# Every third group of value pages summed by VectorE instead of TensorE in the chunk loop of a hybrid decoder step

## Chip, cores and metric

One Trainium2 chip, one core. The metric is the device time of one execution of the whole program in microseconds; lower is better.

## What is computed

The kernel does one inference step of a two-layer decoder for a prompt group (1024 tokens) and eight sample rows with a past of 2048 tokens each. Two parts of the first layer matter here. The samples attend to a paged cache, and the last product of that attention is a weighted sum of 16 value pages of 128 rows for every sample:

```python
k_past = k_pool[page_table].reshape(db, past, HA, 2, DA)
v_past = v_pool[page_table].reshape(db, past, HA, DVA)
...
return jnp.einsum('bhqk,bkhe->bqhe', a.astype(v.dtype), v)
```

The prompt goes through a gated delta rule in chunks, where each chunk needs the inverse of a unit lower triangular matrix and then passes a state on:

```python
v_new = u_c - w_c @ S
o = q_c @ S + attn_c @ v_new
S = S * jnp.exp(gl)[..., None, None] + jnp.einsum('bhck,bhcv->bhkv', k_c, v_new)
```

All is in 32-bit floats.

## The kernel before

The five engines each run one instruction list written out by hand, held together by semaphores. The names: H = 4 heads, NB = 8 chunks of 128 tokens, PG = 16 pages per sample, B = 8 samples, so 128 value pages in all. A group is STRIPS = 4 pages. There are GROUPS = 3 x NB = 24 groups in the chunk loop, which is pages 0 to 95 (samples 0 to 5, LATE = 96). The last 32 pages (samples 6 and 7) are summed in the output projection behind it.

**The chunk loop** (`chunk_pe` from L1890, `chunk_act`, `chunk_dve`) interleaves two chunks in step k = 1 to 8. It finishes the inverse of chunk k-1 (levels 3, 4, 5) and starts that of chunk k (levels 0, 1, 2). A level has a left product on PE, a scaled copy of it on ScalarE (`copy_x`), two right products on PE (`right`, `right_turned`), and two merges on VectorE (`join`, `join_turned`). With the inverse done, chunk k-1 gets its new values (L2012), ScalarE's copy of them (L2177), its outputs (L2022, L2023), the product for the state (L2032) and VectorE's state update (`advance`, L2330). Behind the update come the turned merge of level 2, the mask product `lower` (L2255) for the next chunk, ScalarE's seeds, and the first merge of the next step (`pairs`). PE's keys-times-state product (L2002) waits for the update and the seeds. In step 8 there is no chunk 8, so its levels 0 to 2 are left out, and gates and scales of the first output tiles stand in their place on VectorE (L1785, L1790).

**The value pages** ride along. SP loads pairs of pages into a ring of four slots (`load_pages`, issued at L1142, queued in order), each behind the use of the pair four earlier; `vpage_used` counts pages used, and starts at 8. `page_group` (L1848) sums four pages on PE: four matmuls, each with a page's 128x32 weights on its own 32 columns of the array and the page's 512 values as the moving operand, into one PSUM bank. `group_copy` (L1861 copies, L1864 adds) takes the bank into the sample's `strip_sum` on VectorE. Each step has three such groups: one behind the turned keys, one behind left(k, 1), and the third behind left(k, 2), directly ahead of the outputs. When a sample's four groups are in, `page_column` (L1835) folds the strips into one column per head, four products of a 128x128 stationary operand with one column, in steps 2, 4, 5, 6 and 8 (`SAMPLE_AT`), ahead of right_turned(k, 1). The column of sample 5 stands behind the first output job. `page_column_in` (L1868) copies a column out.

**Behind the loop**, `page_sum` (L1405 for a first page, L1407 for the others) sums the pages of samples 6 and 7 on VectorE: four multiply-adds of 128x128 per page, one per head, into an accumulator `pacc`. SP's list there is: two pairs of pages, then the parked residual (L1823, L1825), which waits for the last state update, then the other pairs with output weights (L1813) between them. PE runs the output jobs (L2406, eight 128x344 products of two passes each); job J waits for VectorE's addition (L2543) of job J - 4, and between the jobs stand small products such as L1774 and L2426.

Of the kernel before, what the change touches and what calls it, by code (L numbers as in the profile page):

```python
# [40 lines left out]
PG = 16  # L41
# [128 lines left out]
def build(nc, a, o):  # L170

    with ExitStack() as ctx:
# [6 lines left out]
        bank = ctx.enter_context(nc.psum_tensor("bank", [P, 8, 512], F32))  # L179
# [1213 lines left out]
        def page_sum(dve, g):  # L1393

            b, pp, u = g // PG, g % PG // 2, g % 2
            if u == 0:
                dve.wait_ge(page_in[pp % 4], b * 64 + (512 + 32 * (pp // 4 + 1)))
            dve.wait_ge(vpage_used, 8 + g)
            dve.sem_inc(wait_carrier, 1)
            for h in range(H):  # L1400
                v = (ring if b < B - 2 else ring_last)[:, pp % 4, u, h * P:(h + 1) * P]
                at = g * H + h
                w, d = aw_flat[:, at:at + 1], pacc[b - LATE // PG][:, h, :]
                if g % PG == 0:
                    last = dve.tensor_scalar(d, v, w, None, ALU.mult)  # L1405
                else:
                    last = dve.scalar_tensor_tensor(d, v, w, d, ALU.mult, ALU.add)  # L1407
            last.then_inc(vpage_used, 1)
# [170 lines left out]
        def over(where, n):  # L1579
            return where[:, 512 * n:512 * (n + 1)].rearrange("p (h t) -> p h t", h=H)  # L1580
# [13 lines left out]
        vb = [rb4(14), rb4(15)]  # L1594
        tmp_flat = tmp[:].rearrange("p s c -> p (s c)")
        k_last = big[:, 7 * TT:7 * TT + T]
        pacc = [over(k_last, 0), over(k_last, 1)]
        ring_last = tiles(0, 4)[:, :, 0:T].rearrange("p s (u n) -> p s u n", u=2)
        rows_first = wring[:, 0, 0:H, :]
        rows = [prod[:, 512 * n:512 * (n + 1)].rearrange("p (h t) -> p h t", h=H) for n in range(2)]  # L1600
# [21 lines left out]
        STRIPS = 4  # L1622
# [2 lines left out]
        SAMPLE_AT = {2: 0, 4: 1, 5: 2, 6: 3, 8: 4}  # L1625
        group_in = sem("group_in")
        strip_sum = [flat(16 * TT, H, P), flat(16 * TT + 512, H, P)]

        KK, QK, VT, KT = 1, 2, 3, 4

# [194 lines left out]
            sp.dma_start(res_b[:, k0:KD, chunk(c)], src[:, k0:KD, chunk(c)]).then_inc(x_back, 16)  # L1825

        def page_column(pe, b, n):
            strips = b < LATE // PG
            if strips:
                pe.wait_ge(group_in, PG // STRIPS * (b + 1))  # L1830
            else:
                pe.wait_ge(vpage_used, 8 + PG * (b + 1))
            part = strip_sum[b % 2] if strips else pacc[b - LATE // PG]
            for h in range(H):
                mm = pe.matmul(bank[:, n, h:h + 1], part[:, h, :], fold[:, h:h + 1] if strips else ones[:, 0:1], start=True, stop=True)  # L1835
            mm.then_inc(samp_full, 1)

        def page_group(pe, g, n):

            b, at = g * STRIPS // PG, g * STRIPS  # L1840
            for q in range(STRIPS):
                pp, u = (at + q) % PG // 2, q % 2
                if u == 0:
                    pe.wait_ge(page_in[pp % 4], b * 64 + 512 + 32 * (pp // 4 + 1))
            for q in range(STRIPS):
                pp, u = (at + q) % PG // 2, q % 2
                w = aw_flat[:, (at + q) * H:(at + q) * H + 32]
                mm = pe.matmul(bank[32 * q:32 * (q + 1), n, :], w, ring[:, pp % 4, u, :], start=True, stop=True)  # L1848
            mm.then_inc(vpage_used, STRIPS)

        def group_copy(dve, g, n):

            b = g * STRIPS // PG
            dve.wait_ge(vpage_used, 8 + STRIPS * (g + 1))
            d, src = strip_sum[b % 2].rearrange("p h e -> p (h e)"), bank[:, n, :]
            if g % (PG // STRIPS) == 0:
                if b >= 2:
                    dve.wait_ge(samp_full, b - 1)
                else:
                    dve.wait_ge(bias_io, 64)  # L1860
                dve.tensor_copy(d, src).then_inc(group_in, 1)  # L1861
            else:
                dve.wait_ge(group_in, g)
                dve.tensor_tensor(d, d, src, ALU.add).then_inc(group_in, 1)  # L1864

        def page_column_in(dve, b, n):
# [17 lines left out]
        def chunk_pe(pe):  # L1884
# [55 lines left out]
            def first(c):  # L1940
                if not live(c):
                    return
                pe.wait_ge(inv0, c + 1)
                if c >= 2:
                    pe.wait_ge(inv_up[c % 2], ps(c - 2, NL - 1, True))
                    pe.wait_ge(group_in, 3 * (c - 1))
                for h in range(H):
                    mm = pe.transpose(own(c, 1)[:, h, :], inv[c % 2][:, h, :], ident[:, :])
                mm.then_inc(m0_full, 1)
# [104 lines left out]
            for k in range(1, NB + 1):  # L2054
# [41 lines left out]
                    pe.wait_ge(x_copied[(k - 1) % 2], xs(k - 1, NL - 1))  # L2096
                    page_column(pe, SAMPLE_AT[k], 2 * ((k + 1) % 2))
                right_turned(k, 1)
                pe.wait_ge(group_in, 3 * k - 2)
                values_new(k - 1)  # L2100
                left(k, 2)
                page_group(pe, 3 * (k - 1) + 2, 2 * ((k - 1) % 2) + 1)
                pe.wait_ge(group_in, 3 * k - 1)
                outputs(k - 1)
                right(k, 2)
                right_turned(k, 2)
# [128 lines left out]
        def chunk_dve(dve, step):  # L2235
# [118 lines left out]
            for k in range(1, NB + 1):  # L2354
# [19 lines left out]
                group_copy(dve, 3 * (k - 1) + 1, 6)  # L2374
                join(k, 1)
                join_turned(k, 1)
                join(k, 2)
                advance(k - 1)
                join_turned(k, 2)
                lower(k + 1)  # L2380
                group_copy(dve, 3 * (k - 1) + 2, 2 * ((k - 1) % 2) + 1)
                if k in SAMPLE_AT:
                    page_column_in(dve, SAMPLE_AT[k], 2 * ((k + 1) % 2))

# [1473 lines left out]
```

## Time and profile before

| | us |
|---|---|
| median of 3 runs (2678.0 to 2679.62) | 2678.15 |
| the profiled execution | 2680.63 |
| its span | 2678.8 |
| PE busy in the span | 2628.7 (98%) |
| VectorE busy | 1524.4 (57%) |
| ScalarE busy | 1143.8 (43%) |
| GpSimd busy | 1349.5 (50%) |

The span is the time between the first and the last instruction in the trace. PE is TensorE's matmuls and PEld its weight loads; DVE is VectorE, ACT is ScalarE, POOL is GpSimd and SP is the engine that issues most DMAs (SPq is its queue). A matmul of 32-bit floats shows as two instructions, so a group of four is "x8". PE is busy for 98% of the span, but that is an average over stages: the long matmul streams of the later layers fill most of the span, and the chunk loop with its many short waits takes from about 572 to 745 us. What a change in the chunk loop is worth is read from that stretch and from the output projection behind it, 744 to 877 us.

### The profile page before, as it was taken

The page shows a single profiled execution, that of the slowest core. Times are in us where ns is not written, and L with a number is a line of the kernel's source. Part 1 is how long each engine was busy: PE and PEld are TensorE (multiplying, and loading weights), DVE is VectorE, ACT ScalarE, POOL GpSimd, SP SyncE. Part 2 cuts the span into 40 slices and gives each one's busy share as a digit, 9 for nine tenths or more (in the row PEclk, how much of TensorE's full clock was granted, in tenths as well). Part 3 has the DMA queues.
Part 4 walks back from the last instruction along what each step waited for, and adds up shares of the span by engine and source line. Part 5 has one row for each costly group of instructions (what it writes and reads, how often), then busy time and mean ns, then how long its engine had stood idle before and what let it go on. Part 6 is the DMA issues. An engine that isn't in the chain of part 4 may idle for free.

```text
span 2678.8 us, 46845 instructions
## 1 busy us (share of the span) xinstructions
PE 2628.7 (98%) x17261; PEld 2397.3 (89%) x17261; DVE 1524.4 (57%) x2930; ACT 1143.8 (43%) x1771; POOL 1349.5 (50%) x613
## 2 busy tenths in 40 slices
PE   8999999989999999999999999999999999999998
PEld 5886666667766999999999999999999999999998
DVE  4227868865567333333337885378863788635323
ACT  2227739955523433333233434344343433444333
POOL 0210015611001666667666677676866767665753
PEclk9999999989999999999999999999999999999999
DMA  5220057635683544444444444544444444444553
GB/s 184 69 95 9 17 167 220 206 97 157 174 274 115 149 137 139 142 142 142 141 142 131 138 142 133 144 141 134 142 126 142 142 137 140 134 133 135 155 153 95
DMA packets 457192, 369.00 MB, mean 138 GB/s; under 512 B 15501, under 2 KB 400114, under 8 KB 456732
## 3 DMA queue, kind: packets, MB, share of 16 engines
q1 hardware_dynamic: 444846, 347.05, 44.0%
q0 software_dynamic: 2992, 12.26, 1.5%
q10 hardware_dynamic: 9174, 7.22, 0.9%
q8 instruction: 122, 2.00, 0.3%
q14 instruction: 58, 0.48, 0.1%
HBM read 351.17 MB, written 17.14 MB: 137 GB/s over the span
## 4 chain that ended last, share of the span: by engine, by line
PE 69%; DVE 3%; ACT 1%; DMA 1%; issue 1%; POOL 0%; SPq 0%; DVEq 0%; ACTq 0%
PE bank L2914 21%; PE bank L2916 21%; PE bank L2915 21%; PE bank L2406 4%; DVE tmp L2782 1%; DVE bank L3495 1%; PE bank L1957 1%; ACT tmp L2774 1%; DMA big<-in_cache_attn_v 1%; DMA wring<-in_ffn_w_up 0%; PE bank L2790 0%; PE bank L1848 0%; PE bank L1774 0%; PE bank L3698 0%; POOL wl L3373 0%
## 5 line engine op out<-in xcount | busy, mean ns | idle before, releaser
L3373 POOL TENSOR_TENSOR wl<-wring,wh 128x1024 fp32r<-128x1024 f32 x466 | 1140.1, 2463 | 586.9 <-ACT wh L3130 586.8
L2914 PE MATMUL bank<-xh,wh 128*128 128x344 f32 x2688 | 862.2, 321 | 0.3 <-POOL wl L3373 0.3
L2916 PE MATMUL bank<-xh,wl 128*128 128x344 f32 x2688 | 858.4, 319 | 0.0
L2915 PE MATMUL bank<-xl,wh 128*128 128x344 f32 x2688 | 856.8, 319 | 0.0
L3130 ACT ACTIVATE wh<-wring 128x1024 fp32r<-128x1024 f32 x466 | 484.2, 1055 | 766.9 <-PE bank L2916 635.1
L2914 PEld LDWEIGHTS bank<-xh,wh 128*128 128x128 f32 x2688 | 505.5, 188 | 1.8 <-POOL wl L3373 0.6
L2915 PEld LDWEIGHTS bank<-xl,wh 128*128 128x128 f32 x2688 | 504.1, 188 | 1.2
L2916 PEld LDWEIGHTS bank<-xh,wl 128*128 128x128 f32 x2688 | 505.0, 188 | 0.0
L3451 DVE TENSOR_TENSOR bank<-bank,gates_tmp 128x344 f32<-128x344 f32 x132 | 69.1, 524 | 512.7 <-PE bank L2916 420.4
L3495 DVE SCALAR_TENSOR_TENSOR bank<-big,vec,bank 128x344 f32<-128x344 f32 (+1 forms) x696 | 354.0, 570 | 0.5
L2914 PE MATMUL bank<-hh,wh 128*128 128x344 f32 x1040 | 334.2, 321 | 3.5 <-DVE hl L3453 3.5
L2915 PE MATMUL bank<-hl,wh 128*128 128x344 f32 x1040 | 332.2, 319 | 0.0
L2916 PE MATMUL bank<-hh,wl 128*128 128x344 f32 x1040 | 331.1, 318 | 0.0
L3460 DVE TENSOR_TENSOR res_b<-res_b,bank 128x344 f32<-128x344 f32 x528 | 264.4, 508 | 103.3 <-PE bank L2916 101.4
L2914 PEld LDWEIGHTS bank<-hh,wh 128*128 128x128 f32 x1040 | 195.8, 188 | 5.7 <-DVE hl L3453 5.3
L2915 PEld LDWEIGHTS bank<-hl,wh 128*128 128x128 f32 x1040 | 195.4, 188 | 0.4
L2916 PEld LDWEIGHTS bank<-hh,wl 128*128 128x128 f32 x1040 | 195.6, 188 | 0.0
L1230 PE MATMUL bank<-res_b,wring 128*128 128x344 f32 x576 | 171.5, 452 | 0.0
L3139 ACT ACTIVATE gates_tmp<-bank 128x344 f32<-128x344 f32 x132 | 60.3, 457 | 243.0 <-PE bank L2916 242.9
L1230 PEld LDWEIGHTS bank<-res_b,wring 128*128 128x128 f32 x576 | 109.2, 190 | 57.5 <-issue 1.6
L1358 POOL TENSOR_TENSOR res_a<-ident,sq 128x512 f32<-128x512 f32 x8 | 8.3, 1046 | 185.1 <-PE bank L902 165.6
L1428 DVE TENSOR_TENSOR big<-big,bank 128x1024 f32<-128x1024 f32 x64 | 77.7, 1216 | 26.7 <-DMA big<-in_cache_attn_k 21.3
(443 smaller groups left out, 3119.5 us busy)
## 6 DMA issues: line engine op xcount, KB each, us to landing
wring<-in_ffn_w_down SPq DMA_DIRECT2D x132, 512.0 KB, 3.6
wring<-in_ffn_w_gate SPq DMA_DIRECT2D x131, 512.0 KB, 3.9
wring<-in_ffn_w_up SPq DMA_DIRECT2D x131, 512.0 KB, 3.9
wring<-in_conv_w_pw SPq DMA_DIRECT2D x72, 512.0 KB, 4.0
big<-in_cache_attn_k SPq DMA_DIRECT2D x128, 256.0 KB, 3.0
big<-in_cache_attn_v SPq DMA_DIRECT2D x128, 256.0 KB, 3.0
wring<-in_w_in SPq DMA_DIRECT2D x20, 512.0 KB, 4.0
park<-res_a SPq DMA_DIRECT2D x1, 4128.0 KB, 12.6
```

What stands on the lines that cost most here:

```text
L1230: mm = pe.matmul(bank[:, J % 4, 0:CH], wring[:, n % 4, k, :], res_b[:, k, chunk(c)], start=(k == 0), stop=(k == KD - 1))
L1428: step.lagged(dve.tensor_tensor(ring[:, pp % 4], ring[:, pp % 4], bank[:, 6 + b % 2, :].unsqueeze(1).to_broadcast([P, 2, 512]), ALU.mult))
L2406: mm = pe.matmul(bank[:, J % 4, 0:CH], w[:, k, :], mix[:, k, chunk(c)], start=(k == 0), stop=(k == KD - 1))
L2914: pe.matmul(bank_out, h, mh, start=(n == 0), stop=False)
L2915: pe.matmul(bank_out, h, ml, start=False, stop=False)
L2916: mm = pe.matmul(bank_out, l, mh, start=False, stop=(n == len(terms) - 1))
L3130: act.activation(wh[s % 6][:, :], raw_w[s % WQ] if where is None else where, ACT.Copy).then_inc(wh_done, 1)
L3139: act.activation(gates_tmp[:, t, :], job_bank(off(p, i) + o), ACT.Silu).then_inc(free[0], 1)
L3373: pool.tensor_tensor(wl[s % 6][:, :], raw_w[s % WQ] if raw is None else raw, wh[s % 6][:, :].bitcast(F32), ALU.subtract).then_inc(w_cut, 1)
L3451: step(dve.tensor_tensor(d, d, gates_tmp[:, t, :], ALU.mult))
L3460: dve.tensor_tensor(d, d, job_bank(J), ALU.add).then_inc(free[J % 2], 1)
L3495: step.lagged(dve.scalar_tensor_tensor(s if q < CW - 1 else d, src, col, s, ALU.mult, ALU.add))
```

## The change

The third group of each step leaves PE. Its four pages are summed by VectorE with `page_sum`, three pages between the merges of level 1 and the merge of level 2, and one between that merge and the state update. In step 8, where the merges of levels 1 and 2 do not exist, the four calls stand back to back ahead of the state update. The accumulator of samples 0 to 5 lies in `tmp`. A sample's column is now the sum of two parts, so `page_column` has eight products instead of four, two per head in one PSUM accumulation. The counts of `group_in` follow (two groups per step), the wait on it in `first` goes, and `page_group` waits until the pages ahead of it are used.

```diff
@@ page_sum
+            first = g == STRIPS * first_of(b, False)
+            if first and 2 <= b < 6:
+                dve.wait_ge(samp_full, b - 1)
             dve.wait_ge(vpage_used, 8 + g)
...
-                w, d = aw_flat[:, at:at + 1], pacc[b - LATE // PG][:, h, :]
-                if g % PG == 0:
+                w, d = aw_flat[:, at:at + 1], pacc[b][:, h, :]
+                if first:
...
-        pacc = [over(k_last, 0), over(k_last, 1)]
+        pacc = 3 * [over(tmp_flat, 0), over(tmp_flat, 1)] + [over(k_last, 0), over(k_last, 1)]
...
+        def on_pe(g):
+            return g < GROUPS and g % 3 < 2
+        def pe_groups(g):
+            return sum(on_pe(n) for n in range(g))
+        def first_of(b, pe):
+            return next(g for g in range(b * PG // STRIPS, (b + 1) * PG // STRIPS) if on_pe(g) == pe)
@@ page_column
-            strips = b < LATE // PG
+            pe.wait_ge(vpage_used, 8 + PG * (b + 1))
+            strips = pe_groups((b + 1) * PG // STRIPS) if b < LATE // PG else 0
             if strips:
-                pe.wait_ge(group_in, PG // STRIPS * (b + 1))
-            else:
-                pe.wait_ge(vpage_used, 8 + PG * (b + 1))
-            part = strip_sum[b % 2] if strips else pacc[b - LATE // PG]
+                pe.wait_ge(group_in, strips)
             for h in range(H):
-                mm = pe.matmul(bank[:, n, h:h + 1], part[:, h, :], fold[:, h:h + 1] if strips else ones[:, 0:1], start=True, stop=True)
+                mm = pe.matmul(bank[:, n, h:h + 1], pacc[b][:, h, :], ones[:, 0:1], start=True, stop=not strips)
+                if strips:
+                    mm = pe.matmul(bank[:, n, h:h + 1], strip_sum[b % 2][:, h, :], fold[:, h:h + 1], start=False, stop=True)
@@ page_group
+            pe.wait_ge(vpage_used, 8 + at)
@@ group_copy
-            if g % (PG // STRIPS) == 0:
+            if g == first_of(b, True):
...
-                dve.wait_ge(group_in, g)
+                dve.wait_ge(group_in, pe_groups(g))
@@ first
-                    pe.wait_ge(group_in, 3 * (c - 1))
@@ chunk_pe, step k
-                pe.wait_ge(group_in, 3 * k - 2)
+                pe.wait_ge(group_in, 2 * k - 1)
                 values_new(k - 1)
                 left(k, 2)
-                page_group(pe, 3 * (k - 1) + 2, 2 * ((k - 1) % 2) + 1)
-                pe.wait_ge(group_in, 3 * k - 1)
+                pe.wait_ge(group_in, 2 * k)
                 outputs(k - 1)
@@ chunk_dve, step k
                 join_turned(k, 1)
+                for n in range(3):
+                    page_sum(dve, STRIPS * (3 * k - 1) + n)
                 join(k, 2)
+                page_sum(dve, STRIPS * (3 * k - 1) + 3)
                 advance(k - 1)
                 join_turned(k, 2)
                 lower(k + 1)
-                group_copy(dve, 3 * (k - 1) + 2, 2 * ((k - 1) % 2) + 1)
```

## Rows read from the trace of the kernel before

**Rows 1.** The head of the page.

```profile
span 2678.8 us, 46845 instructions
```

**Rows 2.** The chain of waits, chunk loop: start us, us, what.

```profile
696.59 0.98 PE bank L1835 x8
...
699.88 0.99 PE bank L1848 x8
...
708.24 0.10 issue
```

**Rows 3.** Timeline of step 5: start us, us, engine, line, operation, tiles, count, idle before.

```profile
675.41 1.16 PE L2012 MATMUL bank<-res_b 128*128 128x128 f32 x8
...
676.61 0.60 ACT L2177 ACTIVATE res_b<-bank 128x512 f32<-128x512 f32 x1 [3.45 <-PE bank L2012]
...
677.11 1.07 PE L1848 MATMUL bank<-big,aw 128*32 128x512 f32 x8
...
678.11 0.49 PE L2022 MATMUL bank<-wring,state 128*128 128x128 f32 x2
...
680.94 0.42 DVE L2271 COPY_PREDICATED res_b<-merge,bank 128x256 f32<-128x256 uint8 x1 [4.80 <-PE bank L1957]
...
682.47 1.12 DVE L2330 SCALAR_TENSOR_TENSOR state<-state,rstd,bank 128x128 f32<-128x128 f32 x4 [1.11 <-PE bank L2032]
```

**Rows 4.** Timeline of step 3, no column; step 1 shows the same pattern.

```profile
631.38 0.60 ACT L2177 ACTIVATE res_b<-bank 128x512 f32<-128x512 f32 x1 [2.33 <-PE bank L2012]
...
632.38 1.06 PE L1848 MATMUL bank<-big,aw 128*32 128x512 f32 x8
...
633.37 0.49 PE L2022 MATMUL bank<-wring,state 128*128 128x128 f32 x2
...
636.20 0.43 DVE L2271 COPY_PREDICATED res_b<-merge,bank 128x256 f32<-128x256 uint8 x1 [4.16 <-PE bank L1957]
```

**Rows 5.** Timeline of step 7, no column.

```profile
719.53 0.60 ACT L2177 ACTIVATE res_b<-bank 128x512 f32<-128x512 f32 x1 [2.51 <-PE bank L2012]
...
721.03 0.49 PE L2022 MATMUL bank<-wring,state 128*128 128x128 f32 x2
...
723.86 0.43 DVE L2271 COPY_PREDICATED res_b<-merge,bank 128x256 f32<-128x256 uint8 x1 [4.38 <-PE bank L1957]
```

**Rows 6.** Page sums: the line's instructions (ns), and two stretches of the timeline.

```profile
L1407 DVE SCALAR_TENSOR_TENSOR big<-big,aw x120: 342/345/353, 749.1 to 821.2; 128x128 f32<-128x128 f32 x120
...
792.50 1.14 DVE L1407 SCALAR_TENSOR_TENSOR big<-big,aw 128x128 f32<-128x128 f32 x4
793.79 3.70 DVE L1407 SCALAR_TENSOR_TENSOR big<-big,aw 128x128 f32<-128x128 f32 x12 [0.15 <-DVE big L1407]
...
747.02 1.94 DVE L1405 TENSOR_SCALAR big<-big,aw 128x128 f32<-128x128 f32 x4
```

**Rows 7.** Timeline of step 8.

```profile
741.69 0.49 PE L2022 MATMUL bank<-res_b,state 128*128 128x128 f32 x2 [1.34 <-DVE big L1864]
...
744.77 1.25 DVE L2330 SCALAR_TENSOR_TENSOR state<-state,res_b,bank 128x128 f32<-128x128 f32 x4 [3.14 <-PE bank L2032]
...
746.10 0.39 SPq L1823 DMA_DIRECT2D res_b<-park  x1
```

**Rows 8.** Windows (after the bounds: us; PE, PEld, DVE, ACT, POOL busy; PEclk; DMA share; GB/s), chain, timeline.

```profile
745.00:765.00 20.00, 20.00 (x83) 13.63 (x82) 7.40 (x27) 4.35 (x10) 4.27 (x5) 1.00 1.01 310
...
769.00:770.00 1.00, 1.00 (x2) 0.70 (x3) 1.00 (x5) 0.00 (x0) 0.00 (x0) 0.50 0.66 207
...
751.77 13.96 DMA big<-in_cache_attn_v
...
766.26 1.84 PE L2426 MATMUL bank<-small,big 128*128 128x2 f32 x16
...
768.89 6.50 PE L2406 MATMUL bank<-res_a,big 128*128 128x344 f32 x16 [0.79 <-DVE res_b L2543]
...
777.65 4.73 PE bank L2406 x16
```

## The prediction

> **What bounds the kernel now.** I read the chain of waits first. Through the chunk loop (about 572 to 745 us of the span) it is nearly all PE: the four matmuls of a page group stand in it with 1.00 us (0.99 in the row shown), a page column with 0.98, and the step boundary with a 0.10 us gap in front of the keys-times-state product [rows 2]. So one microsecond of PE work in a step is worth up to one microsecond, and nothing else here is. Next, the timeline of three kinds of step, to see what PE would wait for once the third group is gone [rows 3 to 5]. Then the page sums of the later stage, which price the new VectorE work [rows 6]. Last, the eighth step and the output projection behind it, where the order changes: PE waits for VectorE there, and the DMA engines are full [rows 7, 8].
>
> The sum is made against the profiled span of 2678.8 us [rows 1]; that execution took 2680.63 us, 1.83 us around the span, and the median of the runs is 2678.15. I add the difference to the median. About 0.2% (5.4 us) is what a measurement of this kernel can tell from no change.
>
> **What goes, what comes.** Per step, PE loses one page group (four 512-column matmuls on four column groups, 1.00 us), and VectorE loses the copy of it. VectorE gets four pages of four scalar_tensor_tensor each. PE gets, in every page column of b below 6, four more 128x128 products with a one-column operand; they are the same kind as the four there, so 0.98 us more [rows 2]. Four such columns lie in steps 2, 4, 5 and 6, one in step 8, one behind the first output job. The SP queue is unchanged in order. The new and the dropped waits cost nothing by themselves: the page group's new wait on the pages before it is met a third of a step earlier, and the wait dropped in front of the transposed seed was long met. The dropped copy stood between the mask product and the first merge, and that merge waits for ScalarE's seeds anyway, so it gives nothing in steps 1 to 7.
>
> **Price of a page.** Twelve scalar_tensor_tensor (three pages) take 3.70 us, one page alone 1.14 [rows 6]. So pages follow at 1.28 us (3.70 less 1.14, halved), of which 0.15 is the wait on the page before. An instruction starts some 0.08 before the end printed for the one ahead (rows overlap so throughout). Three pages hence push the next VectorE instruction to 3.54 us after the end printed for the merge before them (3.70 less 0.08 twice), and a lone page holds the engine for 1.05 (1.14 less 0.08, rounded down). These rows read and write the same kinds of tiles, with full DMA beside them, so I take them, not the slowest row: the four multiplications of a first page once took 1.94 us together, beside DMA issues of the GpSimd queue [rows 6]; that is the upper bound for a page. The lower bound is the 1.05 of a lone page.
>
> The Trainium skill ("VectorE: DVE Perf Modes", the section on the TRN2 errata) gives such an SBUF instruction 58 cycles plus one per element at 0.96 GHz, which makes 194 ns (an estimate from that page) where the row shows 345 ns busy. By the page's figure a page would take 0.78 us, every window below would hold, and the whole sum would come to about -2.3 us; the trace does not agree, and the sum goes by the trace.
>
> **Steps with a page column (2, 4, 5, 6).** Before: the new values start at 675.41, left(k,2) at 676.50, the page group at 677.11, the outputs at 678.11, 2.70 us after the new values [rows 3]. After: the column's extra 0.98 us comes first. Then, without the group, the outputs wait for ScalarE's copy of the new values, which ends 1.80 us after their start (676.61 + 0.60 - 675.41); with 0.06 for the semaphore, 1.86. The step changes by +0.98 - (2.70 - 1.86) = +0.14 us. VectorE: the turned merge of level 1 now ends about 676.95 (its product ends where the new values start, now 676.39; the merge starts some 0.13 behind that and is 0.43 long), three pages let the level-2 merge start at 680.49, and its product is there at 680.94 + 0.14 = 681.08. It fits by 0.59. The last page: the level-2 merge starts 1.53 us before the state update (680.94, 682.47), of which it holds the engine 0.35; with 1.05 for the page that is 1.40. It fits by 0.13. So four times +0.14: **+0.56**.
>
> **Steps 1 and 3, without a column.** PE waits for the level-1 merge already, the group follows at 632.38, the outputs at 633.37; ScalarE's copy of the new values ends at 631.98, so the group's whole 0.99 us goes [rows 4]. But the turned merge of level 1 ends at 632.04 (636.20 less the 4.16 idle), three pages reach to 635.58, and the level-2 product is there at 636.20 - 0.99 = 635.21: 0.37 late. The last page's 0.13 of room gives back a part, and the state update comes 0.24 late. Is that on the path? Before, the update is followed by the turned merge, the mask product, ScalarE's seeds and PE's keys-times-state with 0.1 to 0.2 us of PE idle, so yes. Gain 0.75 each: **-1.50**.
>
> **Step 7.** The copy of the new values ends at 720.13, so the outputs go from 721.03 to about 720.17, 0.86 earlier. The merges end at 719.48 (723.86 less the 4.38 idle), three pages reach to 723.02, the product is there at 723.00: even. **-0.86** [rows 5].
>
> Steps 1 to 7: -1.80 us.
>
> **Step 8.** Here the order bites. There is no level 1 or 2 for a chunk 8, so the four pages stand back to back in front of the state update. PE's outputs wait for VectorE's copy of group 22 (until 741.69, some 0.05 after the copy's end) [rows 7]; that copy depends on gates and scales ahead of it, not on group 23, so the dropped group gains nothing, and the longer column, with the new values behind it, ends before 741.7 too: 0. VectorE's pages start at 741.56 and four take 3 x 1.28 + 1.14 = 4.98; the state update starts at 746.46 instead of 744.77, say +1.68. Who waits for that: SP's load of the parked residual, queued behind the state update (746.10, 0.08 after it ended) with all later value pages behind it, and the GpSimd queue's 2 MB state load [rows 7]. The DMA engines are 1.01 busy from 745 to 765 [rows 8], so a burst that starts 1.68 later ends 1.68 later. It is on the path: the chain has 13.96 us of waiting for a value page, then two page sums, an addition, and PE's output job 4 [rows 8]. PE itself is there at 768.10 (766.26 + 1.84), or 769.08 with the column's extra 0.98, well before 768.89 + 1.68 = 770.57. So the extra column of this stage is hidden by the wait, and the shift is **+1.68**. Behind job 4 PE never waits again up to the end of the projection, so nothing absorbs it and nothing adds.
>
> Output job 4 ran in part at half clock: 0.50 granted (1.2 GHz) from 769 on, after two-column matmuls and the 0.79 us wait, and 6.50 us where a later job took 4.73 [rows 8]. I leave that as it is; it may go or grow by its 1.77 us. The Trainium skill ("TensorE: Matmul & The Clock Gate", Part 1) has the clock follow how busy the array has lately been; by that rule a longer wait in front of job 4 brings the same fall at least, so +0 to +1.7 and no gain. The trace shows this one fall only.
>
> **Sum:** -2.36 + 0.56 + 1.68 = -0.12 us. Predicted 2678.0 us, no change that can be measured.
>
> **Rivals.**
> *Slower: page sums overrun their window inside the loop.* Place: between the turned merge of level 1 and the state update, steps 1 to 7. With d more per page than 1.28, steps 1, 3 and 7 lose 4d each, the four column steps about 4d - 0.59, step 8 4d: 32d - 2.4 on top of the forecast. It decides (5.4 us) from d = 0.25, a page of 1.53 us. At the 1.94 of the slow first page (0.80 over the 1.14 of a lone one) it is +23.1 us, 2701.1. For it: the room is 0.59 at best and none in three steps. Against: 120 instructions between 342 and 353 ns [rows 6], and GpSimd's work in the loop lies outside this window. Chance 0.10.
> *Slower, below the bound: the half clock stretches, or the burst ends later than its start moved.* +1.7 to +3.4: 2680 to 2682. Chance 0.14.
> *A small gain: the burst is not held up, or page sums pipeline as a lone page does.* With pages at 1.05 throughout, steps 1 and 3 gain 0.99 each (-2.3 for steps 1 to 7), and step 8 loses 1.0: -1.3; with the clock fall gone too, -3.1; with no shift of the burst, -4.1. 2674 to 2677. Chance 0.14.
> *Faster: the whole third group counts and the added column products hide.* Eight times 1.00 us: 2670.1. Against: the column stands in the chain with its full 0.98 [rows 2], and in step 8 PE waits for VectorE. Chance 0.06.
> *The change does not do what it says:* if the pages for VectorE were late, PE's groups would have waited for them before; no group does. I give it nothing.
> The forecast itself, -1.5 to +1.5: 0.56.
>
> **How the numbers follow.** No change: 0.56 + 0.14 + 0.14 = 0.84; slower 0.10, faster 0.06. Range 2674 to 2683: the small-gain case down to -4.1, and up over the clock case with the beginning of the overrun; left out are the whole gain and most of the overrun, about 0.15.
>
> **What the profile after would show.** Page groups 16 instead of 24; 16 scalar_tensor_tensor per step, 345 ns each, 3.70 us for three pages; page columns of 16 products, 1.96 us. Between state updates: 22.5 us with a column, 21.0 for step 3. VectorE idle in front of the level-2 merge 0.6 us in column steps, none in steps 1 and 3. The last state update near 744.65 (-1.8, +1.7), the parked load right behind it, the DMA wait still about 14 us. Wrong if a page takes over 1.5 us in the loop, if steps with a column grow by over 0.5, or if output job 4 starts more than 3 us away from 768.9.

## The result and the profile after

The changed kernel has a median of 2682.78 us over 20 executions (2678.86 to 2686.57), the kernel before one of 2678.10 over 20 (2673.62 to 2682.10). The ratio is 1.0016, with an interval of 1.001 to 1.0023: slower by 2.7 to 6.2 us, the whole interval on one side. That is under the 0.2% that the prediction called the limit, and just inside its range (2674 to 2683), but no change was forecast and there is one. The profiled execution took 2683.33 us, 0.55 above its median. That of before stood 2.5 above its own, so the two profiles differ by some 2 us less than the medians do.

The head of the page after:

```profile
span 2681.5 us, 46970 instructions
PE 2630.7 (98%) x17245; PEld 2407.3 (90%) x17245; DVE 1553.4 (58%) x3050; ACT 1143.7 (43%) x1771; POOL 1349.4 (50%) x613
```

PE lost eight page groups and is nevertheless busy for 2.0 us more than before. A busy time that grows while its work shrinks says that the work ran slower. The windows between state updates of the kernel after, steps 2 to 8 (behind the bounds: us; PE, PEld, DVE, ACT, POOL busy; granted PEclk; DMA share; GB/s):

```profile
592.09:615.98 23.89, 23.64 (x362) 19.92 (x360) 15.51 (x47) 11.08 (x41) 2.40 (x3) 0.93 0.56 162
615.98:636.72 20.74, 20.13 (x346) 16.62 (x344) 15.36 (x48) 11.08 (x41) 2.40 (x3) 1.00 0.50 143
636.72:660.74 24.02, 23.60 (x362) 19.87 (x360) 15.77 (x48) 11.08 (x41) 2.40 (x3) 0.93 0.56 165
660.74:686.04 25.30, 25.10 (x362) 21.38 (x360) 15.57 (x47) 11.19 (x41) 2.40 (x3) 0.87 0.47 137
686.04:708.62 22.58, 22.11 (x362) 18.55 (x360) 15.57 (x47) 11.08 (x41) 1.89 (x2) 1.00 0.46 131
708.62:728.40 19.78, 18.97 (x338) 15.66 (x336) 14.42 (x43) 10.72 (x40) 1.28 (x1) 1.00 0.83 241
728.40:749.46 21.06, 18.37 (x196) 14.14 (x193) 14.49 (x43) 9.51 (x30) 0.00 (x0) 0.92 0.70 208
```

The column to read with the first is PEclk. The steps with a page column are 2, 4, 5, 6 and 8. Four of them have a granted clock of 0.87 to 0.93, and step 6, with the same 362 PE instructions as steps 2, 4 and 5, has 1.00 and is the only one near the forecast (22.58 us for 22.5). Step 6 is therefore the price of such a step at full clock, and steps 2, 4 and 5 lost 1.31, 1.44 and 2.72 us against it, together 5.47. Before, a step with a column had 1.00 (one shown, step 5):

```profile
660.10:682.47 22.37, 22.17 (x362) 17.81 (x360) 11.98 (x33) 11.18 (x41) 2.40 (x3) 1.00 0.55 157
```

The timeline of PE in step 5 after shows where inside the step:

```profile
673.83 0.68 PE L1972 MATMUL bank<-res_b 64*64 64x64 f32 x16
674.45 0.38 PE L1848 MATMUL bank<-ones,tmp 128*128 128x1 f32 x2
...
676.03 0.55 PE L1850 MATMUL bank<-fold,big 128*128 128x1 f32 x2
676.51 1.12 PE L1972 MATMUL bank<-res_b 64*64 64x64 f32 x16
677.55 2.07 PE L2027 MATMUL bank<-res_b 128*128 128x128 f32 x8
679.56 1.12 PE L1972 MATMUL bank<-res_b 64*64 64x64 f32 x16
680.61 0.79 PE L2037 MATMUL bank<-wring,state 128*128 128x128 f32 x2
...
683.12 0.39 PE L2037 MATMUL bank<-wring,state 128*128 128x128 f32 x2
```

The same kind of matmul, 16 instructions of 64 moving columns, takes 0.68 us ahead of the page column and 1.12 behind it; the last pair of the page column itself already takes 0.55. The new values (L2027) take 2.07 where they took 1.16 before [rows 3], and a pair of the outputs 0.79 where it took 0.49. Near 683 the rate is back. The windows over this stretch say the same of the clock:

```profile
676.30:678.30 2.00, 2.00 (x21) 1.87 (x21) 0.65 (x3) 0.00 (x0) 0.00 (x0) 0.50 0.68 180
678.30:680.30 2.00, 2.00 (x21) 1.77 (x21) 1.83 (x8) 0.60 (x1) 0.00 (x0) 0.50 0.70 220
680.30:682.30 2.00, 2.00 (x16) 1.88 (x13) 1.14 (x4) 1.57 (x7) 0.00 (x0) 0.50 0.06 15
```

PE is busy in every microsecond, and the granted clock is 0.50, the 1.2 GHz level. Step 2 is the same in small; its first window is the column itself, at full clock:

```profile
605.80:607.60 1.80, 1.80 (x20) 1.79 (x16) 1.80 (x7) 0.00 (x0) 0.00 (x0) 1.00 0.52 143
607.60:609.60 2.00, 2.00 (x22) 1.87 (x22) 0.89 (x4) 0.00 (x0) 0.00 (x0) 0.55 0.75 172
```

**A sum over the loop.** From the first group copy of step 1 to the start of output job 5 both kernels do the same work. Before it is 578.94 to 777.51, 198.57 us; after 578.37 to 780.29, 201.92: +3.35. By steps 1 to 8: -0.99, +1.52, -0.97, +1.65, +2.93, -0.12, -0.44 and +1.68, together +5.26, and -1.91 between the last update and job 5. This stretch is the measure in all that follows ("the loop stretch"), since the start of the loop itself moves from one execution to the next (576.5 to 587.0) in code that is the same. Its weak side is that it is set against one single profile of before. Over all ten runs the difference of the medians is 0.0 to 3.3 us above that of the loop stretch, 2.2 in the mean (the change itself: +4.68 for +3.35). So the 198.57 us of before are probably some 2 us more than that kernel usually takes there, and each loop-stretch difference below flatters its kernel by about as much. That profile has the low clock at output job 4, which costs 1.63 us; whether this is the reason is not shown.

The end of the loop and output job 4, timeline after:

```profile
744.57 1.13 DVE L1410 SCALAR_TENSOR_TENSOR tmp<-big,aw,tmp 128x128 f32<-128x128 f32 x4
745.85 3.69 DVE L1410 SCALAR_TENSOR_TENSOR tmp<-big,aw,tmp 128x128 f32<-128x128 f32 x12 [0.15 <-DVE tmp L1410]
749.46 1.12 DVE L2344 SCALAR_TENSOR_TENSOR state<-state,res_b,bank 128x128 f32<-128x128 f32 x4
...
750.65 0.39 SPq L1838 DMA_DIRECT2D res_b<-park  x1
...
769.87 2.43 DVE L1410 SCALAR_TENSOR_TENSOR big<-big,aw 128x128 f32<-128x128 f32 x8 [13.19 <-DMA big<-in_cache_attn_v]
...
773.30 4.87 PE L2422 MATMUL bank<-res_a,big 128*128 128x344 f32 x16
```

Four pages stand in front of the update, the parked load is right behind it, and VectorE waits 13.19 us for a value page. Job 4 starts without a wait and takes 4.87 us; before it waited 0.79 and took 6.50 [rows 8].

### The profile page after: what moved, and what is told of

Same layout as the page of the kernel before. It is cut to its first block, busy times and chain, and to the rows that moved or that the text cites. A ratio compares the mean times of both kernels' runs of the same rounds, so it can differ in the third digit from the quotient of the medians.

```text
span 2681.5 us, 46970 instructions
## 1 busy us (share of the span) xinstructions
PE 2630.7 (98%) x17245; PEld 2407.3 (90%) x17245; DVE 1553.4 (58%) x3050; ACT 1143.7 (43%) x1771; POOL 1349.4 (50%) x613
## 4 chain that ended last, share of the span: by engine, by line
PE 92%; DVE 3%; ACT 2%; DMA 1%; issue 1%; SPq 0%; POOL 0%; DVEq 0%; ACTq 0%
PE bank L2930 21%; PE bank L2932 21%; PE bank L2931 21%; PE bank L1230 6%; PE bank L2422 4%; PE bank L1972 2%; PE bank L922 2%; PE bank L372 1%; PE bank L524 1%; PE bank L523 1%; PE bank L522 1%; PE bank L902 1%; PE bank L873 1%; DMA wring<-in_w_in 1%; PE bank L1864 1%
```

## The experiments

A page column of the changed kernel is eight products, which the profile shows as 16 matmul instructions; one before the change is four, or eight instructions. Where the expectations say sixteen products, they count these instructions.

Two theories at first. **Theory A:** the longer page column, 16 instructions in a row with one moving column each, makes the clock fall. **Theory B:** the dropped page group (four matmuls of 512 moving columns behind the new values) was what kept the clock up. Each experiment changes one of the two.

**The column's products with 128 moving columns.** The same 16 instructions in number; only the width of the moving operand differs.

```diff
@@ page_column, b < 6
-                mm = pe.matmul(bank[:, n, h:h + 1], pacc[b][:, h, :], ones[:, 0:1], start=True, stop=not strips)
-                    mm = pe.matmul(bank[:, n, h:h + 1], strip_sum[b % 2][:, h, :], fold[:, h:h + 1], start=False, stop=True)
+                    pe.matmul(b4(n)[:, h, :], pacc[b][:, h, :], ones[:, :], start=True, stop=False)
+                    mm = pe.matmul(b4(n)[:, h, :], strip_sum[b % 2][:, h, :], fold[:, h:h + 1].to_broadcast([P, P]), start=False, stop=True)
@@ page_column_in
-            dve.tensor_copy(sacc[:, b * H:(b + 1) * H], bank[:, n, 0:H]).then_inc(sacc_done, 1)
+            src = b4(n)[:, :, 0] if b < LATE // PG else bank[:, n, 0:H]
+            dve.tensor_copy(sacc[:, b * H:(b + 1) * H], src).then_inc(sacc_done, 1)
```

> The changed kernel, but each product of the columns of samples 0 to 5 has 128 moving columns instead of 1 (same sums, copied out of the first column). Theory A: sixteen products with one moving column keep PE nearly idle in what the clock looks at, and that is why the granted clock fell to 0.5 behind four of five columns (excess over my forecast 1.38, 1.51, 2.79 and 0.07 us in steps 2, 4, 5, 6). Then the clock stays at 1.00 behind every column, the state updates of column steps are 22.6 to 22.9 us apart (16 x 0.136 = 2.2 us of column for 1.96), the loop is about 4.5 us shorter than the changed kernel's, and the median 2 to 4.5 us lower (less if the clock falls again at output job 4, +1.6). Theory B: it fell because the 512-column page group behind the column is gone; then the falls stay and the steps stay at 23.9 to 25.3.

Measured: ratio 1.0009 (1.0 to 1.0018), median 2680.12 us; loop stretch 198.30, which is -0.27 to before and 3.62 shorter than with the change, where 4.5 was expected. Step 5 in the windows, and output job 4:

```profile
664.19:686.87 22.68, 22.21 (x362) 18.55 (x360) 15.58 (x47) 11.07 (x41) 2.39 (x3) 1.00 0.52 150
...
773.98 6.56 PE L2425 MATMUL bank<-res_a,big 128*128 128x344 f32 x16 [0.86 <-DVE res_b L2562]
```

All steps have a clock of 1.00 here, and the four column steps take 22.68 or 22.69 us. The page group is as absent as in the changed kernel, so B falls. The expectation's reason for A, that PE is nearly idle in what the clock looks at, is not shown by this or any later run. The 128-fold moving operand costs 0.10 us a step: step 6 of the changed kernel, at full clock, took 22.58. Job 4 shows the low clock again, behind a wait of 0.86 us, as before the change.

**One part of the column only** (the output lacks VectorE's part of six samples).

```diff
@@ page_column
-                mm = pe.matmul(bank[:, n, h:h + 1], pacc[b][:, h, :], ones[:, 0:1], start=True, stop=not strips)
-                if strips:
-                    mm = pe.matmul(bank[:, n, h:h + 1], strip_sum[b % 2][:, h, :], fold[:, h:h + 1], start=False, stop=True)
+                if not strips:
+                    mm = pe.matmul(bank[:, n, h:h + 1], pacc[b][:, h, :], ones[:, 0:1], start=True, stop=True)
+                else:
+                    mm = pe.matmul(bank[:, n, h:h + 1], strip_sum[b % 2][:, h, :], fold[:, h:h + 1], start=True, stop=True)
```

> The changed kernel without the products of VectorE's part in the columns of samples 0 to 5 (that part of the attention is left out of the output), so a column is four products again, 0.98 us, and the third page group stays off PE. Theory A: no clock fall behind any column, column steps 21.5 us apart, the median 8 us below the changed kernel. Theory B: falls stay, column steps over 22.5.

Measured: ratio 0.9991 (0.9982 to 1.0001); loop stretch 194.43, -4.14. Steps 5 and 8, ScalarE's copy of the new values, the first output of step 5 and that of step 8:

```profile
657.20:678.89 21.69, 21.22 (x354) 17.66 (x352) 15.49 (x48) 11.07 (x41) 2.40 (x3) 1.00 0.57 161
720.50:741.57 21.07, 17.48 (x188) 13.21 (x185) 14.50 (x44) 9.50 (x30) 0.00 (x0) 0.92 0.68 202
...
673.70 0.60 ACT L2192 ACTIVATE res_b<-bank 128x512 f32<-128x512 f32 x1 [3.45 <-PE bank L2028]
...
674.56 0.46 PE L2038 MATMUL bank<-wring,state 128*128 128x128 f32 x2 [0.28 <-ACT res_b L2192]
...
736.80 0.49 PE L2038 MATMUL bank<-res_b,state 128*128 128x128 f32 x2 [2.46 <-DVE big L1881]
```

No page group, a short page column, and the clock stays at 1.00 in steps 2, 4, 5 and 6, at 21.69 us each. So the four added products cost 0.89 us at full clock (22.58 of the changed kernel's step 6 less 21.69), where the prediction had 0.98 from the whole column of before.

Step 8 doesn't fit theory A: its page column is the short one, and its clock is 0.92. There PE stands still for 2.46 us behind the new values, and the low clock comes about a microsecond behind that wait. In step 8 PE waits 0.57 to 2.46 us in every profile; the clock fell in both profiles of the change, here, in two of the three with the column in halves below, and in none of the five of before, the doubled kernel and the wide column. A length of the wait doesn't sort these: 1.56 us stands both in the changed kernel, which fell, and in the wide one, which didn't. Step 8 is left out of the counts below for this reason.

**The kernel before with each column product issued twice.** The page group is there; only the column is longer.

```diff
@@ page_column (kernel before)
-                mm = pe.matmul(bank[:, n, h:h + 1], part[:, h, :], fold[:, h:h + 1] if strips else ones[:, 0:1], start=True, stop=True)
+                for _ in range(2 if strips else 1):
+                    mm = pe.matmul(bank[:, n, h:h + 1], part[:, h, :], fold[:, h:h + 1] if strips else ones[:, 0:1], start=True, stop=True)
```

> The kernel before, with every product of the columns of samples 0 to 5 issued twice into the same place (same result), so a column is 1.96 us, and the page groups all on PE. Theory A: clock falls to 0.5 behind most columns, column steps 22.4 + 1.0 + 1.4 to 2.8 = 24.8 to 26.2 us, the median 5 to 12 us above the kernel before. Theory B: no falls, column steps 23.35, the median +4 us (four columns in the loop; the other two hide).

Measured: ratio 1.0028 (1.0018 to 1.0037), the slowest of all; loop stretch 203.80, +5.23. Steps 2 and 4:

```profile
592.98:616.23 23.25, 23.06 (x370) 18.71 (x368) 11.99 (x31) 11.16 (x41) 2.40 (x3) 1.00 0.56 156
...
637.95:662.75 24.80, 24.61 (x370) 19.40 (x368) 12.00 (x32) 11.17 (x41) 2.40 (x3) 0.93 0.49 143
```

Steps 4 and 5 fall to 0.93 (24.80 and 24.77 us), steps 2 and 6 don't (23.25 and 23.58 us, each 0.88 above before). "Behind most columns" was expected, and it is two of four. The group behind the new values doesn't prevent the fall; whether it makes it rarer, two of four can't tell. For steps 2, 4, 5 and 6, A stands by all three.

**The wide column, and step 8's pages behind the state update.** This takes the second loss, step 8's 1.68, too.

```diff
@@ chunk_dve, on top of the wide column
-                for n in range(3):
+                for n in range(3 if k < NB else 0):
                     page_sum(dve, STRIPS * (3 * k - 1) + n)
                 join(k, 2)
-                page_sum(dve, STRIPS * (3 * k - 1) + 3)
+                if k < NB:
+                    page_sum(dve, STRIPS * (3 * k - 1) + 3)
                 advance(k - 1)
+                for n in range(0 if k < NB else STRIPS):
+                    page_sum(dve, STRIPS * (3 * k - 1) + n)
```

> As wide, and in step 8 the last state update stands ahead of the four page sums. If the +1.68 us of step 8 was the pages in front of the state update, the interval between the last two state updates is 19.4 us instead of 21.06, the parked load starts 1.7 us earlier, and with the clock held the whole is 1.5 us below wide and at or a little below the kernel before (-0.1 to -2.5 us). If the output projection is bound by PE's own chain from the first output job on, it equals wide within 0.5.

Measured: ratio 1.0003 (0.9994 to 1.0012); step 8 takes 19.38, as before the change, 1.69 less than with the wide column alone; the loop stretch 197.61, -0.96. Only 0.69 of the 1.69 shows there. The timeline at sample 5's column:

```profile
748.82 0.49 PE L1849 MATMUL bank<-ones,tmp 128*128 128x128 f32 x2 [1.60 <-DVE tmp L1410]
```

The column stands behind the first output job and now waits 1.60 us for the four pages that moved. A step later in VectorE's list became a wait in PE's. The earlier state update by itself gives PE nothing: from the first group copy to the first output job it takes 164.28 us for 164.15 with the wide column alone. What it gives comes at output job 4, which starts without its wait of 0.86 us and takes 4.87 us for 6.56; the 1.60 is lost against that.

**The column in two halves.** Its VectorE part stays at the old place ahead of the turned product, the strips' part goes behind left(k, 2); the halves are added when the column is copied out. Sixteen instructions with one moving column as in the change, but no longer in a row: some 2.3 us of other products stand between the two eights.

```diff
@@ chunk_pe
-                    page_column(pe, SAMPLE_AT[k], 2 * ((k + 1) % 2))
+                    page_column(pe, SAMPLE_AT[k], 2 * ((k + 1) % 2), (0,))
                 right_turned(k, 1)
...
                 left(k, 2)
+                if k in SAMPLE_AT:
+                    page_column(pe, SAMPLE_AT[k], 2 * ((k + 1) % 2), (1,))
@@ page_column_in
+                last = dve.tensor_reduce(d, bank[:, n, 0:2 * H].rearrange("p (two h) -> p h two", two=2), AX.X, ALU.add)
```

> The changed kernel with the column in two halves of four one-column products: VectorE's part where the column stood, the strips' part behind left(k, 2), in the place of the dropped page group, each into its own four PSUM columns, added as they are copied out. If it is the length of an unbroken run of one-column products that brings the clock down, the clock stays at 1.00 though as many of them are issued, and column steps are 22.3 us apart (21.69 of the kernel with one part, plus 0.98 less the 0.35 that PE waits for ScalarE's copy there); the loop is 7 us shorter than the changed kernel's, the median 3 to 6 us lower. If it is their number in a step, the falls stay.

Measured: ratio 0.9999 (0.9991 to 1.0008); loop stretch 196.38, -2.19. Steps 5 and 8:

```profile
659.84:682.10 22.26, 22.07 (x362) 18.55 (x360) 15.48 (x47) 11.19 (x41) 2.40 (x3) 1.00 0.58 156
...
723.92:745.86 21.94, 19.13 (x195) 15.16 (x192) 14.59 (x44) 9.50 (x30) 0.00 (x0) 0.85 0.72 212
```

The column steps keep 1.00 and take 22.26 or 22.27 us, 0.31 less than at full clock with the column in a row: the second half stands where PE would wait 0.28 us for ScalarE's copy. In step 8 there is no left(k, 2), only the new values stand between the halves, and the clock is 0.85 there; PE also waits 1.67 us behind them, and no run separates the two. Against the change the loop stretch is 5.54 us shorter, where 7 was expected, and the median 3.8 lower, where 3 to 6 was.

**The halves, step 8's pages behind the update, and sample 5's column behind the second output job.**

```diff
@@ chunk_dve: as in the wide column with step 8's pages behind the update
@@ behind the loop, on top of the halves
             job_out(0)
-            page_column(pe, B - 3, 5)
             gn_turn(0)
             job_out(1)
+            page_column(pe, B - 3, 5)
```

> As split, with the last state update ahead of the four page sums of step 8, and the column of sample 5 behind the second output job instead of the first, where PE waited 1.6 us for those sums. Expected: last interval 19.4 us, no wait of PE on VectorE up to output job 4, job 4 in 4.9 us at full clock; in all 2.5 to 4.5 us below the kernel before. If the output stage gives the loop's gain back again (a later page or residual transfer), it equals the kernel before within 1 us.

Measured: ratio 0.9993 (0.9984 to 1.0001); loop stretch 194.02, -4.55. Step 8, and job 4:

```profile
720.88:740.26 19.38, 16.57 (x196) 12.52 (x193) 10.10 (x27) 9.50 (x30) 0.00 (x0) 1.00 0.69 207
...
764.35 4.87 PE L2434 MATMUL bank<-res_a,big 128*128 128x344 f32 x16
```

Every step has a clock of 1.00, step 8 is as short as before, and job 4 runs at the full rate. The median is 1.7 us below the kernel before, where 2.5 to 4.5 was expected.

**The wide column with the same two moves** tells whether the late column alone gives back what the moved pages lost.

```diff
@@ on top of the wide column with step 8's pages behind the update
             job_out(0)
-            page_column(pe, B - 3, 5)
             gn_turn(0)
             job_out(1)
+            page_column(pe, B - 3, 5)
```

> wide_adv8 with the column of sample 5 behind the second output job. wide_adv8 gained 1.7 us in step 8 and gave it back: PE waited 1.6 us in front of that column. If that wait was the whole of it, this is 1.6 us below wide_adv8 by its profile from the first state update on, and 1 to 2.5 us below the kernel before.

Measured: ratio 0.9996 (0.9987 to 1.0004); loop stretch 195.28, -3.29, which is 2.33 below the same kernel with the early column: the 1.60 wait is gone, and step 7 happens to be 0.51 shorter (19.55 for 20.06). Column steps 22.68, step 8 19.38. The halves beat the wide column by 1.26 in the loop stretch; four times 0.42 would be 1.68, and step 7 was 0.50 longer in that profile of the halves (20.05).

**The changed kernel once more**, for a second profile.

> The changed kernel once more, to see whether the same columns are followed by the low clock. If the fall depends only on what PE does, steps 2, 4 and 5 are long again and step 6 is not. If it also depends on when the run of one-column products comes, another set of the column steps is long: each either 22.7 us or 23.9 to 25.3, at least two of the four long, and the clock 0.5 in those alone.

Measured: ratio 1.0019 (1.001 to 1.0027); loop stretch 200.78, +2.21. Steps 4 and 5:

```profile
645.43:668.01 22.58, 22.11 (x362) 18.57 (x360) 15.77 (x47) 11.06 (x41) 2.40 (x3) 1.00 0.57 161
...
668.01:691.79 23.78, 23.59 (x362) 19.93 (x360) 15.58 (x48) 11.05 (x41) 2.39 (x3) 0.93 0.55 154
```

Again three of four column steps fell, but others: 2, 5 and 6 (23.99, 23.78, 23.77 us), and 4 kept its clock with 22.58 us, the same as step 6 in the first profile; step 8 had 0.84. Which column is hit is not fixed by the program. The profiled execution was the slowest of its twelve (2692.18 us for a median of 2683.28), but its loop stretch is shorter than that of the first profile; what made it slow lies outside the loop.

**The halves with both moves once more.**

> split_adv8_late once more (its first interval against the kernel before was 0.9984 to 1.0001): column steps 22.27, last interval 19.38, no low clock in the loop; the median 1 to 4 us below the kernel before, and 4 to 8 us below the changed kernel beside it.

Measured: ratio 0.9991 (0.9983 to 1.0), loop stretch 196.37, -2.20. The column steps again at 1.00 and 22.24 to 22.26 us. Step 8, though, has 0.86 and takes 21.92 this time, with the same wait of 1.67 us: the fall there comes in some executions.

## Why the prediction was wrong

**The step that failed** is the one on the column: "so 0.98 us more". It took the added products as time at full clock and put the clock behind them at nothing, without a reason. Their time was nearly right (0.89 us). But a page column of 16 instructions with one moving column, 1.9 us in a row, was followed by a granted clock of 0.50 at 8 of the 12 such columns in steps 2, 4, 5 and 6 (three of four in each of the two profiles of the change, two of four in the doubled kernel before). With eight instructions in a row it was none of 8, with 16 of 128 moving columns none of 12, and with two eights and other products between none of 12. Each fall cost 1.19 to 2.72 us; in the profiled execution of the change they are the 5.47 us above, and 3.80 in its second profile. The mean granted clock of all executions agrees for the change: 0.992 over 20 and again over 12, against 0.995 over those of before and over the 11 of the wide column. It is too coarse to sort the others: the doubled kernel, with falls, and the one-part kernel, with none in these four steps, both have 0.994.

The narrow row alone is not enough for the fall. Sample 5's column stands between output jobs of 344 moving columns, and there 16 one-column instructions in a row kept a clock of 1.00 in all six profiles that have them. The rows of 16 two-column instructions ahead of job 4 were followed by the low clock only where PE also waited (0.28, 0.79 and 0.86 us, job 4 in 6.50 or 6.56), and by none where it didn't (eight profiles, 4.87 us). In the loop the neighbours are matmuls of 64 and 128 columns. Whether it is they that matter no run here shows, and the cause of the fall is shown only as far as this: in the loop, the unbroken row and its width of one bring it.

The profile of before gave a hint that I read for job 4 alone. There the half clock stood behind two-column matmuls and a wait, and I put it to the wait as well as to the matmuls. The nearest kind of matmul to the added ones was in that row, and the question whether 16 of them in the loop would do the same was not asked. Nor is it the only fall in that trace, as the prediction has it: ahead of the loop the granted clock is 0.50 from 556 to 560 and from 564 to 572 us, behind waits of PE of 0.8 to 3.7 us.

The Trainium skill ("TensorE: Matmul & The Clock Gate", Part 1) has the clock follow how busy the array has been of late. The windows here show PE busy for 1.80 of 1.80 us in the column, and the clock fell behind it. Whoever applied the page's rule with the busy time of the profile would have forecast no fall, and the runs don't agree with that. At job 4, where the prediction used this rule, its condition didn't come: PE did not wait, and the clock stayed up, which agrees with it.

**The rest of the sum, by its terms.** With the wide column, where the clock holds, the loop stretch came to -0.27 for a forecast of -0.12. That agreement is in part luck: steps 1 to 7 gave -1.38 for -1.80, and of the shift behind step 8, which was to arrive whole, 0.64 didn't: job 4 starts 23.48 us behind the last state update, 24.12 before. The medians, with +2.35 us and an interval from 0 to +4.8, don't confirm it either. The terms:

- *Steps with a column, +0.14 each:* +0.21 at full clock (22.58 against 22.37). The outputs wait for ScalarE's copy as forecast, but start 0.26 us after its end (673.70 + 0.60 to 674.56, one part only; 0.25 in the wide kernel), where 0.06 was allowed for the semaphore. With the 0.09 less for the products, that is the difference but for some hundredths. Step 6 took 22.70 before, more than the other three, and so came out at -0.12; why is not shown. The pages fitted their windows: VectorE waits 0.48 us ahead of the level-2 merge in step 6, and longer where the clock is low (2.94 in step 5).
- *Steps 1 and 3, -0.75 each:* -0.99 and -0.97, the whole group. The prediction took every page as multiply-adds, but the first page of a sample's VectorE part is a plain multiplication (L1408), and so begins six of the eight groups. Its instructions take 277 ns for 347, and three pages with it end 3.43 us after their start instead of 3.69 (timeline of step 3 after, below the list). That takes 0.26 from the 0.37 that the pages were to be late.
- *Step 7, -0.86:* -0.44 in this profile, -0.67 to -0.16 over the others with the change in them. Without it the step's time moves as well (20.22 before, 20.52 in the doubled kernel). Not settled.
- *Page sums:* 345 ns forecast, 347 measured (L1410, 339 to 353, over the 104 multiply-adds in the loop), and 3.69 us for three pages of them. The rival of an overrun has nothing for it.
- *Step 8, +1.68:* +1.68 (21.06 for 19.38). The step was right, for the reason given: four pages in front of the update. The clock was 0.92 in it too, hidden behind VectorE's pages (the wide kernel takes 21.07 at 1.00). In the second profile of the change, at 0.84, it was not hidden: 21.61.
- *The out stage:* the update comes 4.69 us later than before and the value page 3.97 (769.87 for 765.90), so the burst moved with the update but for 0.7. The column of this stage was hidden in the wide kernel, where PE still waits 0.86 us behind it, as forecast; in the changed kernel PE doesn't wait there, and nothing hides it.
- *Job 4, left as it was:* PE came late enough not to wait, and the low clock went: 4.87 us for 6.50, a gain of 1.63 and with the wait 2.42. In the wide kernel, where PE again waited 0.86, it was back with 6.56. The stretch behind the last update came out 1.91 shorter, which covered about a third of the 5.26 lost in the loop.

The first page of step 3 after, the two behind it, and the level-2 merge that follows them:

```profile
631.94 0.86 DVE L1408 TENSOR_SCALAR tmp<-big,aw 128x128 f32<-128x128 f32 x4
632.96 2.41 DVE L1410 SCALAR_TENSOR_TENSOR tmp<-big,aw,tmp 128x128 f32<-128x128 f32 x8 [0.15 <-DVE tmp L1408]
635.29 0.42 DVE L2285 COPY_PREDICATED res_b<-merge,bank 128x256 f32<-128x256 uint8 x1
```

**The rivals.** The one of the half clock had the right resource and nearly the right size (2680 to 2682, with 2682.78 measured), but at output job 4, the one place where the low clock vanished. Its price, +1.7 to +3.4, came from other rows than those that bore it. "The change does not do what it says" and the whole gain of 8 us were rightly set low. That the range held, by 0.2 us, is luck: it reached up to 2683 for a clock fall at job 4 and the beginning of an overrun, and neither came.

**The signs named beforehand.** Page groups 16 (128 matmul instructions of L1864), three pages in 3.69 us and the parked load behind the update were there. Two of the three things that were to prove the forecast wrong came: steps with a column grew by over 0.5 (+1.52, +1.65, +2.93), and job 4 started 4.4 us away from 768.9, with 3 as the limit.

**A better version.** The halves with both moves stand at 0.9993 (0.9984 to 1.0001) and 0.9991 (0.9983 to 1.0) of the kernel before: about 2 us below it, at the edge of what its runs can tell from nothing, and some 7 us below the changed kernel (2676.22 and 2675.66 for 2682.78 and 2683.28).

## What to carry to other kernels

When an edit puts short matmuls in a row on PE, look at the width of their moving operand and not only at their microseconds, and at the granted clock behind the nearest rows of the same kind; a busy PE is no sign that the clock will hold. If the clock falls, put other products between the short ones, or widen their moving operand, which cost 0.10 us for 16 instructions here. The place counts as well: the same row between wide matmuls kept its clock. Price a moved block in both lists: four pages taken out of VectorE's critical stretch came back as a 1.60 us wait in PE's until the consumer moved as well. And when differences of 2 us matter, one profile of the kernel before is not enough to measure all others by.

## What the runs showed that was not expected

- The granted clock fell to the 1.2 GHz level with PE busy without a gap, behind 8 of 12 rows of 16 one-column instructions in the loop, and stayed there for some 3 to 7 us of work with 64 to 128 moving columns. Between output jobs of 344 moving columns it fell behind none of 6 such rows.
- Sixteen matmul instructions of 128x128 with 128 moving columns took hardly longer than with one: 22.68 us a step for 22.58.
- Four products fewer in the column of step 8 didn't keep the clock there: behind a wait of 2.46 us it was 0.92 for the step.
- From the end of ScalarE's copy to the start of PE's matmul that waits for it, 0.26 us pass in the one-part and 0.25 in the wide kernel.
- The doubled column alone, with no other edit, cost 7.5 us in the medians (2685.24 for 2677.77), where its 24 added products (six columns at 0.88 us) are at most 5.3 us at full clock, and those of step 8 are hidden (19.39 us for 19.38).
